# Sample value products of a two-layer attention trunk: per head in two column halves of TensorE instead of per pair of heads

## The reference, cut to what matters

```python
# A, for the sample: q (32 rows), k and v (256 cached + 32 new rows = 288)
w = jnp.where(causal, jnp.exp(log_beta + between), 0.0)     # (B, H, 32, 288)
return jnp.einsum('bhqk,bkhd->bqhd', w.astype(v.dtype), v)  # (B, 32, H, 64)
# B, for the sample
p = jax.nn.softmax(logits, axis=-1)
return jnp.einsum('bqhk,bqkhd->bqhd', p.astype(vs.dtype), vs)
```

## Time and profile before

| | us |
|---|---|
| median of three runs | 1654.52 (1652.79 to 1655.17) |
| profiled execution, its own time | 1654.94 |
| its span in the trace | 1653.1 |
| TensorE busy (matmul) | 1577.2, 95% of the span |
| VectorE busy | 958.3, 58% |
| ScalarE busy | 683.2, 41% |
| GpSimd busy | 629.6, 38% |
| mean granted TensorE clock | 0.985 of full |

### The profile page before, as it was taken

How to read it: one execution, slowest core, us unless ns; L and a number is a source line. 1 busy time by engine, 2 the same in 40 slices (tenths; PEclk the granted TensorE clock), 3 DMA queues, 4 the chain that set the end, 5 groups by cost and what they waited for, 6 DMA issues and landing times.

```text
span 1653.1 us, 29789 instructions
## 1 busy us (share of the span) xinstructions
PE 1577.2 (95%) x11742; PEld 1460.5 (88%) x11742; DVE 958.3 (58%) x1748; ACT 683.2 (41%) x1302; POOL 629.6 (38%) x346
## 2 busy tenths in 40 slices
PE   6999999988999999999999999988899999999998
PEld 5788896768999999999988888876699999999998
DVE  6767666754666256526757677667366651662461
ACT  4325454553444134324433354545444432442342
POOL 5223231334543443434542233223174344443332
PEclk9999998998999999999999999999899999999999
DMA  4433311121233223332242312111132332233223
GB/s 131 140 114 102 101 39 39 53 66 52 78 90 90 86 84 88 90 90 83 76 113 82 102 53 58 43 42 46 54 88 79 90 89 84 85 90 90 87 81 95
DMA packets 243202, 133.99 MB, mean 81 GB/s; under 512 B 10430, under 2 KB 236590, under 8 KB 243062
## 3 DMA queue, kind: packets, MB, share of 16 engines
q1 hardware_dynamic: 243062, 132.08, 27.4%
HBM read 120.14 MB, written 14.24 MB: 81 GB/s over the span
## 4 chain that ended last, share of the span: by engine, by line
PE 70%; DVE 15%; ACT 6%; DVEq 3%; issue 3%; POOL 2%; ACTq 1%; DMA 0%; SPq 0%
PE g_ps L1182 13%; PE g_ps L1183 13%; PE g_ps L1186 12%; PE a_ps L1183 7%; PE a_ps L1186 7%; PE a_ps L1182 7%; DVE score L740 2%; ACT work L991 1%; PE a_ps L1274 1%; POOL w_lo L1688 1%; PE a_ps L1261 1%; DVE prob L1664 1%; DVE top L737 1%; PE a_ps L694 1%; ACT w_hi L898 1%
## 5 line engine op out<-in xcount | busy, mean ns | idle before, releaser
L1688 POOL TENSOR_TENSOR w_lo<-raw,w_hi 128x1024 fp32r<-128x1024 f32 (+2 forms) x210 | 505.3, 2406 | 705.2 <-ACT w_hi L898 705.2
L1182 PE MATMUL g_ps<-h_hi,w_hi 128*128 128x272 f32 (+1 forms) x1616 | 450.0, 296 | 11.2 <-DVEq L1567 5.2
L1183 PE MATMUL g_ps<-h_lo,w_hi 128*128 128x272 f32 (+1 forms) x1616 | 440.0, 291 | 0.0
L898 ACT ACTIVATE w_hi<-raw 128x1024 fp32r<-128x1024 f32 (+2 forms) x210 | 217.6, 1036 | 448.9 <-PE g_ps L1186 313.1
L1186 PE MATMUL g_ps<-h_hi,w_lo 128*128 128x272 f32 (+1 forms) x1616 | 337.4, 290 | 0.0
L1182 PEld LDWEIGHTS g_ps<-h_hi,w_hi 128*128 128x128 f32 (+1 forms) x1616 | 306.6, 190 | 25.4 <-issue 10.4
L1183 PEld LDWEIGHTS g_ps<-h_lo,w_hi 128*128 128x128 f32 (+1 forms) x1616 | 306.5, 190 | 0.6
L1576 DVE SCALAR_TENSOR_TENSOR wts<-work,par,wts 128x546 f32<-128x546 f32 x176 | 201.0, 1142 | 100.0 <-ACT wts L1080 92.5
L1186 PEld LDWEIGHTS g_ps<-h_hi,w_lo 128*128 128x128 f32 (+1 forms) x1616 | 254.8, 189 | 0.0
L1182 PE MATMUL a_ps<-h_hi,w_hi 128*128 128x272 f32 x720 | 194.5, 288 | 0.0
L1183 PE MATMUL a_ps<-h_lo,w_hi 128*128 128x272 f32 x720 | 194.3, 289 | 0.0
(11 more groups left out here) (230 smaller groups left out, 2768.4 us busy)
## 6 DMA issues: line engine op xcount, KB each, us to landing
raw<-in_w_up SPq DMA_DIRECT2D x88, 512.0 KB, 3.7
raw<-in_w_in SPq DMA_DIRECT2D x56, 512.0 KB, 3.6
raw<-in_w_down SPq DMA_DIRECT2D x32, 512.0 KB, 3.7
raw<-in_w_out SPq DMA_DIRECT2D x16, 512.0 KB, 3.7
raw<-in_w_down SPq DMA_DIRECT2D x16, 384.0 KB, 3.4
bias_turns<-bias_line SPq DMA_DIRECT2D x8, 320.0 KB, 4.9
x_nat<-in_x_prompt SPq DMA_DIRECT2D x4, 512.0 KB, 5.9
out_p_av<-v_nat SPq DMA_DIRECT2D x4, 512.0 KB, 5.4
```

Source lines behind the costliest of these rows:

```text
L898: act.activation(w_hi[:, n % SPLIT, 0:kt, 0:c], raw[:, n % RAW, 0:kt, 0:c], ACT.Copy).then_inc(hi_done, 1)
L1182: pe.matmul(g[0:c, a, 0:HALF], w_hi[:, s, j, 0:c], xh[:, mov], start=(j == 0), stop=False)
L1183: pe.matmul(g[0:c, a, 0:HALF], w_hi[:, s, j, 0:c], xl[:, mov], start=False, stop=False)
L1688: pool.tensor_tensor(w_lo[:, s, 0:kt, 0:c], raw[:, n % RAW, 0:kt, 0:c], w_hi[:, s, 0:kt, 0:c].bitcast(F32), ALU.subtract).then_inc(lo_done, 1)
```

## The change

Both sample products go through one new function. Where there was one matmul for a pair of heads, there are now two, one for each head: its own 64 value columns as weights, its own 32 query columns moving, the even head's output in partitions 0 to 63 of a_ps[3] and the odd head's in 64 to 127, both in the same 32 columns of the pair. The key blocks are the outer loop and the two heads the inner one, so that the halves take turns. The output of a product is 128 x 128 without unwanted quarters, and o_evac copies it with one copy. Waits and signals stay as they are.

```diff
+        def sample_values(pe, w, at):
+
+            for p in range(PAIRS):
+                for kb in range(SKB):
+                    r = P if kb < 2 else DEC
+                    for e in range(2):
+                        o = at(p, kb) + e * DEC
+                        mm = pe.matmul(a_ps[3][e * HD:(e + 1) * HD, p * DEC:(p + 1) * DEC], vs_nat[w][0:r, kb, p * P + e * HD:p * P + (e + 1) * HD],
+                                       wts[0:r, o:o + DEC], start=(kb == 0), stop=(kb == SKB - 1), skip_group_check=True)
+            return mm
...
             if h == "s":
-                for e in range(2):
-                    r = slice(e * HD, (e + 1) * HD)
-                    src = a_ps[3][r, 0:PAIRS * 64].rearrange("p (t e q) -> p t e q", t=PAIRS, e=2)[:, :, e, :]
-                    dve.tensor_copy(o_t[r, t0:t0 + PAIRS, SEQ:TOK], src)
+                dve.tensor_copy(o_t[:, t0:t0 + PAIRS, SEQ:TOK], a_ps[3][:, 0:PAIRS * DEC].rearrange("p (t q) -> p t q", t=PAIRS))
...
-                        for p in range(PAIRS):
-                            for kb in range(SKB):
-                                r, o = (P, kb * 256) if kb < 2 else (DEC, 512)
-                                mm = pe.matmul(a_ps[3][:, p * 64:(p + 1) * 64], vs_nat["a"][0:r, kb, p * P:(p + 1) * P], wts[0:r, o + p * 64:o + (p + 1) * 64],
-                                               start=(kb == 0), stop=(kb == SKB - 1))
+                        mm = sample_values(pe, "a", lambda p, kb: (kb * 256 if kb < 2 else 512) + p * 64)
...
-                        for p in range(PAIRS):
-                            for kb in range(SKB):
-                                r = P if kb < 2 else DEC
-                                o = (p // 2) * 384 + kb * P + (p % 2) * 64
-                                mm = pe.matmul(a_ps[3][:, p * 64:(p + 1) * 64], vs_nat["b"][0:r, kb, p * P:(p + 1) * P], wts[0:r, o:o + 64],
-                                               start=(kb == 0), stop=(kb == SKB - 1))
+                        mm = sample_values(pe, "b", lambda p, kb: (p // 2) * 384 + kb * P + (p % 2) * 64)
```

## The result

The changed kernel takes 1646.03 us, median of four runs (1644.79 to 1646.61). The kernel before took 1653.93 beside it (four runs, 1652.79 to 1655.17). The ratio is 0.9948 with a 95% interval of 0.9936 to 0.996: 7.9 us or 0.5% less. The profiled execution took 1645.48 us with a span of 1643.7, 9.4 less than before, at a mean granted clock of 0.988 (0.985 before).

What follows compares the result with a forecast made beforehand. TensorE work, seven tenths of the span, was taken as the bound. A's products 2.5, B's 5.4 and copies 0.6 make 8.5 us off the profiled 1654.9: 1646.4, so a median of 1646.0; range 1642.0 to 1651.0.

Steps and rivals of the forecast that it cites:

- The parts of a product: Both sample products at full clock: load steps, matmul groups and emptying sum to 2.35 us, plus 0.09 in A.
- The loads bind: Within a group of the product, weight loads set the pace: one every 0.055 us in each half, columns 0.03.
- the 0.09 that A was to pay for coming from 128-column weights: At the start of A's product TensorE must empty once more, 0.09 us, making it 2.44; B has no such cost.
- a change of row count costs time of its own: Between 128-row and 32-row groups TensorE empties, 0.15 us after the change; two changes for each pair stay.
- The halves run together: In both products the two heads' loads and matmuls run side by side and count as one, plus 0.01 us.
- the rival in which they take turns: In both products each load waits for the other half's: product 3.6 us, gain 1.1 in all, 1653.4; chance 0.12.
- Slow issue: TensorE's instructions come too slowly: 96 records at 0.0625 us, product 6.0, total 5.2 slower at 1659.7; chance 0.04.
- The copy: One copy of about 0.3 us replaces two taking 0.59; behind B 0.6 less in all, behind A nothing.
- B's product: From first matmul to copy, 5.29 and 5.47 us become 2.4 to 2.9, taken as 2.65: 5.4 less in all.
- The 1.9 us after which the clock was to fall: In B's product the clock may fall 1.9 us in, as before; the remaining 0.5 then takes about 1.0: 2.9.
- the low stretch behind B about as long as before: Half-clock stretch behind B's product, 10.2 and 10.1 us before, keeps about that length; start and end some 3 us earlier.
- The third rival: Same 2.4 us product, but the clock falls earlier or stays low longer and takes gain back: 1650.5; chance 0.09.

Runs made afterwards that it cites:

- the B part alone: New product and its copy in B only, A as before, against the kernel before: 1647.91 us (5 runs), ratio 0.9951.
- the second set of runs: The changed kernel itself, unchanged, run again beside later kernels, against the kernel before: 1647.39 us (5 runs), ratio 0.9954.
- A alone: New product and its copy in A only, B as before, against the kernel before: 1653.59 us (11 runs), ratio 0.9984.
- the kernel with the wide product in two groups: Kernel before, pair-wide weights and two copies kept, all 128-row key blocks first, then all 32-row ones: 1651.67 us (9 runs), ratio 0.9979.
- the filled kernel before: Kernel before plus eight matmuls of 272 columns behind B's product whose result nobody reads: 1654.09 us (11 runs), ratio 0.9996.
- three fillings: Changed kernel with 128-row blocks first, plus unread matmuls: 14 before a norm's reduction, 18 before logits, 8 behind B; 1651.09 us, 0.9979 to kernel before.

## Why the prediction came out right

**The total.** Forecast 1646.0, measured 1646.03. That it fits to 0.03 us is luck: the same kernel beside other runs gave 1647.39, and errors cancel. The profiled execution was forecast at 1646.4 and took 1645.48, and the median was to be 0.4 below it and came 0.55 above. The terms were less exact than the total, too.

**The parts of a product** hold. The loads bind, 0.057 for a step of two where 0.055 was taken, and a product at full clock takes 2.42 to its last end where 2.44 to the next load was forecast (measured so: 2.35). A lost 1.34 each time instead of 1.25. The difference is the 0.09 that A was to pay for coming from 128-column weights: B's product, which had no such cost, takes the same 2.42 us at full clock (the B part alone, layer 0), so no run shows it. That a change of row count costs time of its own is shown by the two kernels with fewer of them, at 0.12 and 0.14 us each.

**The halves run together**; the rival in which they take turns is out, by the 0.14 and 0.31 us above. The Trainium skill, in "TensorE: Matmul & The Clock Gate", section "The mechanism" of Part 3, has loads overlap with matmuls in flight only where their row groups differ. For two column halves in the same 128 rows the trace disagrees: eight loads in 0.31 us, beside matmuls of the same rows. But the orders with the halves apart show that something like the rival's price is real, 2.68 against 1.71 us, and 4.79 against 2.42 where the row count changes twice as often as well. It is the alternation that avoids it.

**Slow issue** is out too: 48 loads and 48 matmuls in 1.71 us are 0.018 for a record.

**The copy** was 0.3 each, in the chain behind B and beside TensorE behind A, as forecast.

**B's product** was to be 2.65 to the copy. Measured are 3.15 and 2.69, inside the 2.4 to 4.3 that was bounded. The 1.9 us after which the clock was to fall were no constant: it fell 1.2 and 2.0 in, and in one run of the B part alone not within the product. So B gave 4.9 and not 5.4.

**The step that failed** is "the low stretch behind B about as long as before". It went from 10.2 to 6.8 us in both layers, the same in the second set of runs, and with A alone it stayed at 10.2. The sum needed another premise, that its end stays where it is relative to the work, and the two don't agree with each other. A stretch that begins some 1.9 us into the product and is as long as before would, behind a product and copy that are 3 us shorter, reach 3 us further into the projection and cost 1.5 us more in each layer. One that ends where it did relative to the projection lasts only about 7 us, which is close to what was measured. The end came 1.8 us earlier in the projection in layer 0 (3.0 us at half instead of 4.8) and at the same place in layer 1 (4.3 both times). So the sum's premise held in one layer and missed 0.9 us in the other, and the early stretch at 48.2 took that back and more. Why the stretch ends where it does is not shown. The prediction took it to hang on the wait at the copy because it was equally long in both layers, but in the kernel with the wide product in two groups it is 10.2 and 6.8 us with the same wait in both.

**The clock's share.** Over the 146 runs that have a clock listed, a run whose mean granted clock was 0.001 above its kernel's mean was 0.8 us shorter (correlation 0.62). The kernel before ran at 0.985 on average (55 runs, mean 1655.0 us), the changed one at 0.988 (9 runs, 1646.6). By that slope 2.5 of the 8.4 us go with the clock, and 5.9 are work at equal clock. This is an estimate: the runs of the kernel before alone have a slope of 0.6, by which it would be 1.9. The edit at full clock gives 4 x 1.34 + 0.6 = 6.0. The third rival had the clock take something back; it gave.

## What to carry to other kernels

Where the load of weights bounds short matmuls and half of the output is thrown away, two column halves with half the columns each cost about 0.6 of the time (2.42 for 3.76 us, 1.71 for 2.92), if matmuls of the two halves alternate one by one; the same matmuls in another order were slower than the kernel before. Put all blocks with the same row count together: each change of it cost 0.12 to 0.14 us here. Read the granted clock behind the changed place too: what a shorter sparse phase gives can be lost or doubled in the dense work that follows, and matmuls that nobody reads may pay (in one kernel of the three here that had them only behind B), but not where they run behind a wait instead of beside it.

## What the runs showed that was not expected

- TensorE overlaps its two column halves only over a short reach: some 0.2 us or four matmuls ahead where 16 matmuls of one half come before 16 of the other.
- The granted clock came back after 3.4, 6.8 or 10.2 us behind B. With TensorE busy throughout (6.65 of 6.70 us) it still stayed low for 6.8, as in the filled kernel before. With three fillings it did not fall at all behind B in layer 1. What tells a stretch of 3.4 from one of 6.8 is open.
- 0.7 to 1.4 us less in each of the four products moved the mean by 1.1 us in all, and eight matmuls behind each B product that nobody reads moved it by 5.7, each known to about 3 us.
